# First norm of a two-block transformer kernel: one token half's squares summed by VectorE, the other half's means placed between product parts

## The reference, cut to what matters

```python
def rms_norm(x, g):
    y = x * lax.rsqrt(jnp.mean(x * x, axis=-1, keepdims=True) + EPS)
    return y * g

def hybrid_layer(x, ...):
    h = rms_norm(x, norm_g)
    u = jnp.einsum('bsd,dc->bsc', h, w_in)
    v_c, b_c, c_c, z_c, q, k, v, z_a, gate_logits = jnp.split(u, SPLIT_POINTS, axis=-1)
    y_c = b_c * causal_depthwise_conv(c_c * v_c, conv_w)
    ...
```

## Time and profile before

| | us |
|---|---|
| median of three runs | 2576.89 |
| lowest and highest of them | 2576.45, 2581.56 |
| the profiled execution's own time | 2580.12 |
| its span, first to last instruction | 2578.2 |
| PE busy | 2517.5 (98% of the span) |
| DVE busy | 1549.4 (60%) |
| POOL busy | 1235.5 (48%) |
| ACT busy | 1125.2 (44%) |

### The profile page before, as it was taken

How to read it: one execution, slowest core, us unless ns; L and a number is a source line. 1 busy time by engine, 2 the same in 40 slices (tenths; PEclk the granted TensorE clock), 3 DMA queues, 4 the chain that set the end, 5 groups by cost and what they waited for, 6 DMA issues and landing times. The chain is left out here.

```text
span 2578.2 us, 36770 instructions
## 1 busy us (share of the span) xinstructions
PE 2517.5 (98%) x11914; PEld 2049.5 (79%) x11914; DVE 1549.4 (60%) x2240; ACT 1125.2 (44%) x2050; POOL 1235.5 (48%) x964
## 2 busy tenths in 40 slices
PE   8999999999999999999999999999999999999998
PEld 5788888887788877888888887778778888878777
DVE  5455542354777776434555555564767777776785
ACT  4333233303765671115777777751433223344432
POOL 3788887443211223432111111136169888666682
PEclk9999999999999999999999999999999999999999
DMA  3222222588100004331111111142033333386552
GB/s 108 86 78 61 65 77 98 200 294 280 54 25 24 29 25 150 128 117 55 38 41 41 41 41 41 62 164 74 24 115 113 115 121 111 126 277 208 181 183 74
DMA packets 126490, 267.18 MB, mean 104 GB/s; under 512 B 13872, under 2 KB 14000, under 8 KB 126400
## 3 DMA queue, kind: packets, MB, share of 16 engines
q1 hardware_dynamic: 84800, 157.85, 19.1%
q10 hardware_dynamic: 41600, 108.19, 11.8%
HBM read 198.02 MB, written 67.96 MB: 103 GB/s over the span
## 5 line engine op out<-in xcount | busy, mean ns | idle before, releaser
L641 POOL TENSOR_SCALAR whi<-raw 128x512 fp32r<-128x512 f32 x194 | 147.1, 758 | 1071.7 <-PE bank L824 647.4
L643 POOL TENSOR_TENSOR wlo<-raw,whi 128x512 fp32r<-128x512 f32 x194 | 275.5, 1420 | 16.2
L761 PE MATMUL bank<-a_hi,whi 128*128 128x512 f32 x464 | 184.7, 398 | 3.5 <-POOL wlo L643 2.0
L761 PE MATMUL bank<-b_lo,whi 128*128 128x512 f32 x464 | 183.4, 395 | 0.0
L656 POOL TENSOR_TENSOR wlo<-a,whi 128x512 fp32r<-128x512 f32 x114 | 166.4, 1460 | 12.8 <-ACT whi L1641 12.1
L824 PE MATMUL bank<-b_hi,whi 128*128 128x512 f32 x384 | 154.9, 403 | 5.6 <-DVE fk_lo_odd L2409 3.2
L824 PE MATMUL bank<-b_hi,wlo 128*128 128x512 f32 x384 | 151.6, 395 | 0.0
L824 PE MATMUL bank<-b_lo,whi 128*128 128x512 f32 x384 | 151.3, 394 | 0.0
L761 PE MATMUL bank<-b_hi,whi 128*128 128x512 f32 x336 | 133.3, 397 | 0.4 <-DVE b_lo L2256 0.3
L761 PE MATMUL bank<-a_hi,wlo 128*128 128x512 f32 x336 | 132.6, 395 | 0.0
L761 PE MATMUL bank<-a_lo,whi 128*128 128x512 f32 x336 | 132.6, 395 | 0.0
(11 more groups left out here) (707 smaller groups left out, 7758.5 us busy)
## 6 DMA issues: line engine op xcount, KB each, us to landing
raw<-in_w SPq DMA_DIRECT2D x206, 256.0 KB, 2.6
a<-in_pairs SPq DMA_DIRECT2D x152, 256.0 KB, 2.6
wd_scr<-wd SPq DMA_DIRECT2D x55, 256.0 KB, 5.4
wd<-in_down SPq DMA_DIRECT2D x44, 256.0 KB, 4.3
xs_scr<-made ACTq DMA_DIRECT2D x40, 256.0 KB, 2.6
fc<-c_scr ACTq DMA_DIRECT2D x16, 512.0 KB, 3.7
h_scr<-up_y ACTq DMA_DIRECT2D x13, 512.0 KB, 2.6
raw<-wd_scr SPq DMA_DIRECT2D x26, 256.0 KB, 2.7
```

The lines of the kernel that those rows point to most:

```text
L641: nc.gpsimd.tensor_scalar(hi, src, 1.0, 1.0, ALU.mult, ALU.mult).then_inc(w_hi, 1)
L643: nc.gpsimd.tensor_tensor(lo, src, hi.bitcast(F32), ALU.subtract).then_inc(w_lo, 1)
L761: last = nc.tensor.matmul(psum_ap, ws[w][:, k, :], a[:, kt, hs(h)], start=(first and i == 0 and j == 0), stop=(final and i == n - 1 and j ...
```

## The change

Four things change, all of them in the first 60 us but for some counters.

- ACT writes the first half's first square straight into `acc`, a row of its own in SBUF, and the other seven into the two `sq` buffers. DVE adds each of these seven to `acc` (new line L2525), and PE makes one mean matmul of the sum (new line L1062) where there were eight. Before each square from the fourth on ACT waits for the add that frees its buffer, no longer for a matmul.
- PE makes the second half's first three means right after that one, and the other five one by one after the product parts k = 0 to 4 of tile 0, first half.
- Tile 1 of both halves goes to `score[0]` and no longer waits on `tile_out`; `first_u` reads it there.
- The counter `first_done` is now also raised by the seven adds, and three later waits on it are raised by 7.

```diff
--- before.py
+++ after.py
@@ -708,7 +708,7 @@
             for i in range(4):
                 split(U_FFN + i, FFN_SLOTS[i], tile_done[i % 2], T_FOUT + 6 + i // 2)
             for c in range(2):
-                split(U_FFN + 4 + c, FFN_SLOTS[2 + c], first_done, 3 + c)
+                split(U_FFN + 4 + c, FFN_SLOTS[2 + c], first_done, KT - 1 + 3 + c)
             for c in range(2):
                 split(U_FFN + 6 + c, FFN_SLOTS[2 + c], tile_done[1], T_FFN + 3 + c)
 
@@ -1058,12 +1058,24 @@
 
             pe.wait_ge(const_made, 3)
 
-            for h in range(2):
-                squares(n0, h, range(KT))
+            pe.wait_ge(first_done, KT - 1)
+            nc.tensor.matmul(score[1][:, hs(0)], feat_mean[:], acc[:, hs(0)], start=True, stop=True).then_inc(n0.sq_used, KT)
+            squares(n0, 1, range(3))
+
+            def first_half(c, h):
+
+                pe.wait_ge(w_lo, c * 2 + 2)
+                dst = score[0][:, hs(h)] if c else bank[h][:]
+                for k in range(KT):
+                    pe.wait_ge(n0.lo, h * KT + k + 1)
+                    last = product(dst, c, a_hi, a_lo, [k], [k], h, k == 0, k == KT - 1)
+                    if c == 0 and h == 0 and k < KT - 3:
+                        squares(n0, 1, [k + 3])
+                last.then_inc(tile_done[h], 1)
 
             for h in range(2):
                 for c in range(2):
-                    half(c, c, c, a_hi, a_lo, h, n0.lo)
+                    first_half(c, h)
             for c in range(2, U_MIX):
                 tile(c, c, c % 2, a_hi, a_lo)
 
@@ -1584,7 +1596,10 @@
 
             nc.scalar.preload_act_table_set("natural_log_exp_and_others")
             for j in range(KT):
-                square(n0, 0, j, False)
+                act.wait_ge(moved[sum(j >= x for x, n in X_PARTS) - 1], 16)
+                if j >= 3:
+                    act.wait_ge(first_done, j - 2)
+                nc.scalar.activation(sq[j % 2][:] if j else acc[:, hs(0)], z[:, j, hs(0)], ACT.Square).then_inc(n0.sq, 1)
             square(n0, 1, 0, False)
             root(n0, 0, eps_rms)
             act.wait_ge(cols_in, 16)
@@ -1940,7 +1955,7 @@
 
                 c, h, f = i % 2, i // 4, i % 4 // 2
                 if f:
-                    act.wait_ge(first_done, 2 * h + 2)
+                    act.wait_ge(first_done, KT - 1 + 2 * h + 2)
                     act.wait_ge(up_conv, 3)
                 else:
                     act.wait_ge(tile_done[c], T_FFN + h + 1)
@@ -2503,6 +2518,11 @@
             v.tensor_scalar(half_gate[:], cst[:, C_GATEB + KT:C_GATEB + 2 * KT], 0.5, None, ALU.mult).then_inc(prepared, 1)
             v.tensor_scalar(shift[:], cst[:, C_LN1B:C_LN1B + KT], ALPHA, None, ALU.mult).then_inc(prepared, 1)
             v.tensor_scalar(neg_sink[:], cst[:, C_SINK:C_SINK + 2 * NPAIR], -1.0, None, ALU.mult).then_inc(chain_step, 1)
+            for j in range(1, KT):
+                dve.wait_ge(n0.sq, j + 1)
+                if j > 1:
+                    dve.wait_ge(first_done, j - 1)
+                v.tensor_tensor(acc[:, hs(0)], acc[:, hs(0)], sq[j % 2][:], ALU.add).then_inc(first_done, 1)
             for h in range(2):
                 scaled_and_lo(n0, h, a_hi, a_lo, C_NORM, None, range(KT))
 
@@ -2585,7 +2605,7 @@
             def first_u(h):
                 dve.wait_ge(tile_out[h], 1)
                 dve.wait_ge(tile_done[h], 2)
-                v.tensor_tensor(cv_u[:, 2 + h * HALF:2 + (h + 1) * HALF], bank[h][:], cv_v[:, hs(h)],
+                v.tensor_tensor(cv_u[:, 2 + h * HALF:2 + (h + 1) * HALF], score[0][:, hs(h)], cv_v[:, hs(h)],
                                 ALU.mult).then_inc(tile_out[h], 1)
 
             def first_by(h):
```

## The result

The changed kernel takes 2586.0 us in the median of seven runs (2583.45 to 2590.57); the kernel before 2578.55 in seven (2573.75 to 2581.56). The ratio is 1.0032 with a 95% interval of 1.0020 to 1.0043: **slower by some 8.2 us** (5.2 to 11.1 by the interval; the two medians differ by 7.45). The profiled execution of the changed kernel took 2585.31 us, its span is 2583.5.

A forecast was written before the change was run, and what follows sets the result against it. PE bounds the kernel, but the low parts' chain sets when tile 0's first half ends. Stalls -1.8, root +0.4 and turns +8.6 give +7.2 us, from the median of 2576.89 to 2584.1; range 2580.5 to 2591.

The forecast's parts named there:

- The closed turns: Tile 0's first half: PE, ACT and VectorE wait in a ring before low parts 2, 3 and 5; +8.6 us.
- The root's start: First half's root after VectorE's sum and one mean: at 17.0 us against 16.60, +0.4 us.
- The turn-taking with GpSimd: VectorE's adds alternate with GpSimd's split of unit 0, so add 7 ends at about 14.3 us.
- the two ends: VectorE's sum of the first half is ready between 12.5 and 14.3 us; 14.3 was taken.
- slow means 9 and 10: Second half's first means still at the slow rate, holding up high part 1: upper bound, +0.8 us.
- The stalls at tile 1: Tile 1 of both halves no longer waits for ACT's copy of tile 0; -1.8 us.
- the cover for the second half's low parts: Tile 0's second half: PE's work just covers the last low part; nothing charged, without it at most 0.3 us.
- TensorE's clock: Rival: TensorE drops to its low level in the turns or never leaves it; +12 to +15 us, chance 0.16.
- The range: Whole kernel: the forecast's own range was 2582 to 2587 us, the overall range 2580.5 to 2591.
- The case without turns: Rival, decided at square 14: means do not hold back ACT's high parts; 2573.7 to 2575.5 us, chance 0.09.
- later by one amount from 60 us on: Sign in the profile after: from 60 us on all as before, shifted by one amount.

The follow-up runs named there:

- e1: Changed kernel with the second half's eight means made before the first product again; ratio to the kernel before 1.0007 (0.9997 to 1.0016).
- e2: Kernel before with only the second half's means 4 to 8 moved behind product parts 0 to 4; ratio to the kernel before 1.0055 (1.0041 to 1.0068).
- e5: Changed kernel with ACT's second root moved from behind high part 4 to behind high part 7; ratio to the kernel before 1.0026 (1.0015 to 1.0036).
- e10: Changed kernel with GpSimd's split of unit 0 held back until the seven adds are done; ratio to the kernel before 1.0036 (1.0023 to 1.0050).
- e3: Kernel before with only tile 1 of both halves put in score[0], without the wait on the copy; ratio to the kernel before 0.9989 (0.9980 to 0.9998).
- e6: Changed kernel with ACT's list alone reordered: high part j before squares 2j+1 and 2j+2, second root behind high part 7; ratio to the kernel before 1.0013.
- e7: e3 with eleven matmuls into an unread bank ahead of the first mean; ratio to the kernel before 0.9992 (0.9983 to 1.0001).
- e11: e7 with the second half's means between the product parts and e6's order on ScalarE; ratio to the kernel before 0.9993 (0.9984 to 1.0002).
- e8: e1 with the same eleven matmuls as e7 ahead of the first mean; ratio to the kernel before 1.0003 (0.9994 to 1.0012).

## Why the prediction was right

It said 2584.1 us, +7.2 against the kernel before, and slower; measured were 2586.0 and 8.2 us, and the mark shows 8.1. By its steps:

- **The closed turns, +8.6: shown, 8.65.** Two turns of 3.84 and 3.85 (3.9 was said) and one of 4.78 (4.6); e1 and e2 show that they come with the interleaving and not with the sum or `score[0]`; e5 opens the third by moving the root, as the list of waits had it. Had I read only the diff, five means would have looked hidden in a stretch where TensorE had waits to spare. What told was the semaphore's count: which mean each square needs, behind which part it stands, and what stands behind that square on ScalarE.
- **The root's start, +0.4: shown.** Adds 4 to 7 ended at 9.90 + 4.40 = 14.30 as worked out, the mean took 2.1 us, the root came at 17.12 (17.0 was said). The turn-taking with GpSimd was the right choice between the two ends, and e10 shows it by taking it away. The Trainium skill's rule that a VectorE instruction with two SBUF inputs and a GpSimd one that reads SBUF exclude each other ("SBUF — State Buffer", "Who interferes with whom") agrees: 3.08 us alone, 4.40 beside it. That this small term held is in part luck: the root of the kernel before stood at 16.60 in one execution, and at 15.48 and 15.66 in e3 and e2, whose start is the same. So is what followed: I allowed 0.8 us for slow means 9 and 10, and the changed kernel paid next to nothing, while e1, with the same lists up to there, was 1.8 late at low part 1 (the changed kernel 0.45).
- **The stalls at tile 1, -1.8: shown**, and the cover for the second half's low parts held as said.
- **TensorE's clock: the term that was missing.** I had it as a rival of 12 to 15 us in which all turns run slow. What came was a part of it, one low stretch behind the last turn, worth 0.9. The mechanism of the rival was right, its size was not: e5 and e10 had one low stretch at another turn, e2 two, worth 0.65 to 1.45 us each, and never did all three turns run slow. The Trainium skill warns that idle gaps between bursts send TensorE to its half clock ("TensorE: Matmul & The Clock Gate", "Why this matters for your kernels"). The 0.51 from 37.4 us on agrees with that; but the page ties it to the length of one gap, and here gaps of the same 2.02 and 2.69 us were followed once by the low level and once not.
- **The range.** From its own lower bounds (1.8 us for the root, 0.9 for the turns) the forecast reaches down to 2581.4, not 2582; nothing else in it hangs on this.
- **The case without turns** fell at the point named: mean 12 was done at 25.6, when VectorE's product for high part 2 had long been made.

Last, "later by one amount from 60 us on" was wrong for the two profiled executions: the shift is 8.2 up to 697 us and 5.0 from 863 on. That is chance in the kernel before, and told below.

## What to carry to other kernels

Before work of engine A is moved behind work of engine B "to fill its gaps", write down for each semaphore count which instruction raises it, and follow one operand once around; if the path comes back to the same engine, the gap is not filled but made longer, here from 1.27 to 3.9 us per step. On an in-order engine it is enough that one instruction in front waits (a square for a buffer) to hold up an unrelated one (the high part). The idle pieces that such a ring makes can also cost TensorE its clock for some us after (here 0.65 to 1.45 us a time). And a single profile is one draw: before a us or two of it is believed, see where its execution lies among the kernel's times. Of this change only the freed bank was worth keeping (e3: 0.9989, 0.9980 to 0.9998).

## What the runs showed of the hardware that I had not expected

**A 0.23 us instruction that takes 1.36.** Of the 3.2 us by which the two profiled executions come closer between 697 and 863 us, each third is one small VectorE instruction. The kernel before, and GpSimd beside it:

```profile
701.87 1.36 DVE L2298 TENSOR_SCALAR neg_max<-mx,neg_sink 128x4 f32<-128x4 f32 x1
```

```profile
701.92 1.29 POOL L643 TENSOR_TENSOR wlo<-raw,whi 128x512 fp32r<-128x512 f32 x1
```

and the changed kernel:

```profile
710.10 0.23 DVE L2313 TENSOR_SCALAR neg_max<-mx,neg_sink 128x4 f32<-128x4 f32 x1
```

```profile
710.15 1.33 POOL L643 TENSOR_TENSOR wlo<-raw,whi 128x512 fp32r<-128x512 f32 x1
```

In both the two start 0.05 us apart; once VectorE waits out all of GpSimd's 1.29, once it doesn't. ScalarE's exponentials and with them TensorE wait behind it. The kernel before met this at 702, 781 and 860 us, the changed one there not once: 3 x 1.13 = 3.4 us of chance. Both met it at three further places (741, 820 and 900 us in the kernel before). Over the eleven traces 3 to 6 of the 32 such instructions are long: six in the kernel before, e1, e2, e3, e6 and e10, five in e5 and e7, four in e11, three in the changed kernel and e8. It is only a part of the scatter: the time less the mark is 2527.0 us with three (the changed kernel) and with six (e10), and largest, 2531.6, with four (e11).

**When TensorE's rate rises is not fixed.** With an unchanged start the first half's means became fast after the fifth square in the kernel before (releases 1.7 us apart up to 11.59) and after the fourth in e2 and e3 (10.01 to 10.98), which moved the root between 15.48 and 16.60. With the sum on VectorE, square 12 is released 7.3 us after the mean on the sum began in the changed kernel, 7.9 in e5, 8.5 in e1, again with the same lists up to there.
